# Twenty weight units multiplied by VectorE instead of TensorE, one matmul for the bias rows, and eight slots for the experts' weights

## What is computed

```python
mod = silu(c) @ w_ada + b_ada              # six passes of 3072 columns over the three blocks
h = modulate(rms_norm(x), shift, scale)
u, q, v, f_f, f_b, g = split(h @ w_in)     # the input layer, 3072 columns, partly for the context too
...                                        # Fourier mixing, and a gated recurrence in both directions
x = x + gate1 * (cat @ w_out)              # the output layer
aff = softmax(h @ w_router); idx = top_k(aff, 32)      # 16 experts, 32 tokens each
hid = silu(x[idx] @ w_g[e]) * (x[idx] @ w_u[e])        # 1024 x 2816 each
ye = hid @ w_d[e]                                      # 2816 x 1024
...                                        # second block: attention, spatial gating, feed-forward
...                                        # third block, two layers: attention with a bias of relative
                                           # positions (rel_bias[bucket(offset)]), short convolution
```

## Time and profile before

| | |
|---|---|
| median of three runs | 2391.78 us |
| the profiled execution: its time / its span | 2389.73 us / 2387.6 us |
| TensorE matmuls busy | 1858.6 us (78%) |
| VectorE busy | 735.8 us (31%) |
| ScalarE busy | 538.3 us (23%) |
| DMA moved | 760.52 MB, mean 319 GB/s |
| mean granted TensorE clock | 0.773 |

### The profile page before, as it was taken

One profiled execution on the slowest core, in us unless ns is written; L12 is line 12 of the kernel. 1 busy time (PEld: TensorE's weight loads), 2 busy tenths in 40 slices (PEclk: granted clock), 3 DMA queues, 4 the chain that ended last, 5 costly groups with the idle time before them and its releaser, 6 DMA issues.

```text
span 2387.6 us, 34411 instructions
## 1 busy us (share of the span) xinstructions
PE 1858.6 (78%) x14680; PEld 1126.4 (47%) x14680; DVE 735.8 (31%) x1170; ACT 538.3 (23%) x860; POOL 54.3 (2%) x70
## 2 busy tenths in 40 slices
PE   5999887676666666766676667667799999999897
PEld 3786752211221122112211211221788899988886
DVE  4216630000000000000000000010655786667767
ACT  3431221000000000000000000000474564464553
POOL 0005000000000000000000000000000000000000
PEclk8999987755665676566657755665899999999998
DMA  8757579999999999999999999999643555743531
GB/s 358 264 196 270 193 304 393 425 425 426 425 426 425 425 426 426 426 425 426 426 426 425 425 425 426 425 426 426 226 133 124 170 173 187 223 147 120 161 102 62
DMA packets 153198, 760.52 MB, mean 319 GB/s; under 512 B 9720, under 2 KB 96504, under 8 KB 99481
## 3 DMA queue, kind: packets, MB, share of 16 engines
q1 hardware_dynamic: 149448, 754.07, 79.2%
q10 hardware_dynamic: 3664, 5.24, 0.6%
HBM read 756.13 MB, written 3.14 MB: 318 GB/s over the span
## 4 chain that ended last, share of the span: by engine, by line
DMA 46%; PE 44%; DVE 5%; ACT 3%; issue 2%; SPq 0%; DVEq 0%; ACTq 0%
PE ps L633 17%; DMA ring<-in_w_exp_down 16%; DMA ring<-in_w_exp_up 15%; DMA ring<-in_w_exp_gate 14%; PE ps L897 7%; PE ps L1020 4%; PE ps L585 3%; PE ps L910 2%; PE ps L552 2%; DMA ring<-in_w_in 1%; PE ps L1002 1%; PE ps L783 1%; DVE ring_lo L1403 1%; PE ps L627 1%; PE ps L964 1%
## 5 line engine op out<-in xcount | busy, mean ns | idle before, releaser
L897 PE MATMUL ps<-ring,arena 128*32 128x352 f32 x4096 | 622.9, 755 | 241.1 <-DMA ring<-in_w_exp_gate 134.1
L897 PEld LDWEIGHTS ps<-ring,arena 128*32 128x32 f32 x4096 | 147.2, 153 | 703.5 <-DMA ring<-in_w_exp_up 257.8
L910 PE MATMUL ps<-ring,arena 128*32 128x256 f32 x2816 | 237.4, 492 | 176.5 <-DMA ring<-in_w_exp_down 129.9
L1403 DVE TENSOR_TENSOR ring_lo<-ring,w_hi 128x1024 fp32r<-128x1024 f32 x220 | 267.7, 1220 | 162.1 <-ACT w_hi L1060 161.0
L633 PE MATMUL ps<-u_hi,w_hi 128*128 128x258 f32 x960 | 278.3, 290 | 3.3 <-DVE ring_lo L1403 3.2
L633 PE MATMUL ps<-u_hi,ring_lo 128*128 128x258 f32 x960 | 272.4, 284 | 0.0
L633 PE MATMUL ps<-u_lo,w_hi 128*128 128x258 f32 x960 | 272.4, 284 | 0.0
L1748 DVE TENSOR_TENSOR arena<-arena,ps 128x704 f32<-128x704 f32 x15 | 13.3, 888 | 776.3 <-PE ps L897 776.3
L910 PEld LDWEIGHTS ps<-ring,arena 128*32 128x32 f32 x2816 | 99.5, 136 | 323.1 <-DMA ring<-in_w_exp_down 183.7
L1060 ACT ACTIVATE w_hi<-ring 128x1024 fp32r<-128x1024 f32 x220 | 230.3, 1050 | 92.7 <-PE ps L1020 36.2
L633 PEld LDWEIGHTS ps<-u_hi,w_hi 128*128 128x128 f32 x960 | 183.1, 191 | 14.4 <-DVE ring_lo L1403 8.8
(11 more groups left out here) (258 smaller groups left out, 1945.3 us busy)
## 6 DMA issues: line engine op xcount, KB each, us to landing
ring<-in_w_exp_gate SPq DMA_DIRECT2D x128, 1408.0 KB, 10.7
ring<-in_w_exp_up SPq DMA_DIRECT2D x128, 1408.0 KB, 10.9
ring<-in_w_exp_down SPq DMA_DIRECT2D x112, 1536.0 KB, 11.5
ring<-in_w_ada SPq DMA_DIRECT2D x48, 1536.0 KB, 8.7
ring<-in_w_in SPq DMA_DIRECT2D x38, 1536.0 KB, 7.2
ring<-in_w_ff SPq DMA_DIRECT2D x18, 1536.0 KB, 7.1
ring<-in_w_out SPq DMA_DIRECT2D x8, 1536.0 KB, 7.3
ring<-in_w_exp_down SPq DMA_DIRECT2D x16, 512.0 KB, 10.5
```

The lines of the kernel that those rows point to most:

```text
L897: m = pe.matmul(ps[32 * j:32 * j + 32, 2 * (k // 8) + i, 0:FJ // 2], XCUR[:, k % 8, :], ring[:, s, at:at + FJ // 2], start=(k % 8 == 0), s ...
L910: m = pe.matmul(ps[32 * j:32 * j + 32, 4, 0:T], HIDT[:, c, :], ring[:, s, at:at + T], start=(c == 0), stop=(c == FC - 1), skip_group_check ...
L1403: tt(slot(c["u"], KD, c["w"], of=ring_lo)[:, :, at], slot(c["u"], KD, c["w"])[:, :, at], w_hi[:, s % HI, :, :].bitcast(F32), ALU.subtract) ...
```

## The change

Three things change together.

**Twenty modulation units go to VectorE.** All of pass 1, all of pass 2 and four units of pass 3 (`DVE_ADA`) are loaded during the input layer, in slots 2 and 3 by turns, while the input layer's own units use slots 0 and 1 by turns. VectorE multiplies each element by the row's condition and adds it to an accumulator of 128 x 3072 (two instructions of 1536 columns a unit, in `add_ada`), right behind the low parts of the same item. `IN1_ADA` says how many such loads follow each of the input layer's units on SP. TensorE then sums each accumulator over the partitions with a matrix of ones, in eight matmuls of 384 columns (`ada_sum`): pass 1 behind item 10 of the input layer, pass 2 behind item 26, pass 3's part behind the layer. The turn of pass 1 comes behind item 12, that of pass 2 behind the layer. The other four units of pass 3 and pass 4 stay on TensorE, between the Fourier and the level steps; pass 5 follows the output layer.

**Bias rows.** One matmul makes all eight heads' rows on eight partitions, and each row is stored by a DMA that reads its one partition 128 times.

**Eight slots.** The experts' units go through eight slots: the four of the ring, one over the buffers of the high parts, three in a region whose data are no longer used by then. Experts' units 0 and 1 are issued ahead of most of pass 5. Slots are no longer `u % 4` but given by lists (`CYCLE`, `EXP_CYCLE`), and a load waits for the unit that had its slot before. The first load of in2 now has slot 0, whose last user is the experts' last unit but one. SP's loop over the experts is written out. The gating weights are loaded behind the experts, and their mask is applied in the second block.

```diff
-BROW_EVERY = 3
+SLOTS_ALL = 8
+CYCLE = (2, 3, 1, 0)
+EXP_CYCLE = (6, 7, 4) + CYCLE + (5,)
+IN1_ADA = [0, 2, 2, 1, 2, 2, 3, 3, 5]
+DVE_ADA = [(1, k) for k in range(KD)] + [(2, k) for k in range(KD)] + [(3, k) for k in range(4)]
+BROW_AT, SUM1_AT, TURN1_AT, SUM2_AT = 4, 10, 12, 26
+ADA_COND = (0, 0, 2, 2, 3, 3)
...
-    def unit(self, dmas=1):
+    def unit(self, dmas=1, by="unit_used", at=None):
+
         u = self.n
         self.n += 1
-        self.fill[u % RING] += 16 * dmas
-        self.ready[u] = self.fill[u % RING]
+        if at is None:
+            at = CYCLE[self.turn % RING]
+            self.turn += 1
+        self.where[u], self.before[u], self.last[at] = at, self.last[at], u
...
+        with nc.sbuf_tensor("w_hi_raw", [P, HI * KD * P], F32) as w_raw_t:
+            w_raw = w_raw_t[:]
         w_hi = sb("w_hi", [P, HI, KD, P], F32R)
...
+        ACC = (ar(0, 2 * ADA_J), tail[:, 0:2 * ADA_J])
+        SLOT = [ring[:, i, :] for i in range(RING)] + \
+            [w_raw[:, 0:UNIT], ar(4 * K1, UNIT), ar(20 * K1, UNIT), ar(23 * K1, UNIT)]
...
             def load(u, dst, src):
-                if u >= RING:
-                    sp.wait_ge(S("unit_used"), u - RING + 1)
-                sp.dma_start(dst, src).then_inc(w_ready[u % RING], 16)
+                if plan.before[u] is not None:
+                    name, n = plan.used[plan.before[u]]
+                    sp.wait_ge(S(name), n)
+                sp.dma_start(dst, src).then_inc(w_ready[plan.where[u]], 16)
...
             def after_in1(i):
-                if i < KD:
-                    load_ada(1, [i])
+                for _ in range(IN1_ADA[i]):
+                    p, k = next(dve_ada)
+                    load_ada(p, [k])
...
-            for p in (2, 3):
-                load_ada(p)
+            load_ada(3, range(4, KD))
+            load_ada(4)
             load_dense(out1, inp["w_out"][0])
-            for p in (4, 5):
-                load_ada(p)
+            load_ada(5, range(1))
...
+            sp.wait_ge(S(plan.used[out1[0]["u"]][0]), plan.used[out1[0]["u"]][1])
+            sp.wait_ge(S("bias_stored"), 16 * ATT)
+            load_expert(0)
+            load_expert(1)
+            load_ada(5, range(1, KD))
+            sp.wait_ge(S(plan.used[out1[-1]["u"]][0]), plan.used[out1[-1]["u"]][1])
+            for i in range(2, 7):
+                load_expert(i)
+            sp.wait_ge(S("xs"), KD)
+            for i in range(7, EXPERTS * EXP_UNITS):
+                load_expert(i)
...
+            def ada_sum(p):
+
+                pe.wait_ge(S("rows_out"), p)
+                pe.wait_ge(S("ada_used"), min(KD * p, len(DVE_ADA)))
+                for i in range(2):
+                    for j in range(CG):
+                        at = ADA_J * (j % 2) + ADA_J // 2 * i
+                        m = pe.matmul(ps[32 * j:32 * j + 32, 6 + i, 0:ADA_J // 2], ones[:, 0:32],
+                                      ACC[j // 2][:, at:at + ADA_J // 2], start=True, stop=(p < 3),
+                                      skip_group_check=True)
+                count(m, "ada_summed")
...
+            for i, _ in enumerate(dense_blocks(in1, in1_src, lat)):
+                if i == BROW_AT:
+                    pe.wait_ge(S("rel_in"), 32)
+                    m = pe.matmul(ps[0:ATT, 5, 0:511], REL[0:33, :], OFFS[0:33, 0:511], start=True, stop=True)
+                    count(m, "brow")
+                if i == SUM1_AT:
+                    ada_sum(1)
+                if i == TURN1_AT:
+                    turn(1)
+                if i == SUM2_AT:
+                    ada_sum(2)
+            turn(2)
+            ada_sum(3)
...
-                fill(2 if n < LEVELS - 1 else 0)
+                fill((1 + n % 2) if n < LEVELS - 1 else 0)
...
-                act.dma_start(scratch[h:h + 1, 0:P * 512].rearrange("a (q j) -> q (a j)", q=P)[:, 0:511],
-                              BROW[:, h % 2, 0:511]).then_inc(S(f"bias_stored{h % 2}"), 16)
+                act.dma_start(scratch[h:h + 1, 0:P * 512].rearrange("a (q j) -> a q j", q=P)[:, :, 0:511],
+                              BROW[h:h + 1, 0:511].unsqueeze(1).broadcast_to([1, P, 511])).then_inc(S("bias_stored"), 16)
...
+                    if BROW_AT < done <= BROW_AT + ATT:
+                        bias_row(done - BROW_AT - 1)
...
+            def add_ada(k):
+
+                for _ in range(k):
+                    p, kc = next(to_add)
+                    u = ada[p][kc]
+                    waits(f"w_ready{plan.where[u]}", plan.ready[u])
+                    c = conds[:, kc, ADA_COND[p]:ADA_COND[p] + 1]
...
+                    for i in range(2):
+                        w = slot(u, ADA_PASS)[:, 2 * ADA_J * i:2 * ADA_J * (i + 1)]
+                        if kc == 0:
+                            ins = ts(ACC[i], w, c, None, ALU.mult)
+                        else:
+                            ins = stt(ACC[i], w, c, ACC[i], ALU.mult, ALU.add)
+                    mark(ins, "ada_used")
+
+            done = 0
+            for gi, g in enumerate(in1):
+                share = IN1_ADA[gi + 1] if gi + 2 < len(in1) else (3, 2)[gi + 2 - len(in1)]
+                for i, it in enumerate(g["items"]):
                     low_parts(it["s"] + HI)
-
+                    n = len(g["items"])
+                    add_ada(share * (i + 1) // n - share * i // n)
+                    if done == TURN1_AT + 1:
+                        mod_in(1)
+                    done += 1
+            waits("ada_summed", 3)
```

More of the change, by code:

```diff
@@ L120, in __init__ @@
         self.ready = {}
-        self.fill = [0] * RING
+        self.fill = [0] * SLOTS_ALL
+        self.last = [None] * SLOTS_ALL
+        self.before = {}
+        self.where = {}
+        self.used = {}
+        self.counts = {"unit_used": 0, "ada_used": 0}
+        self.turn = 0
         self.blocks = 0
@@ L124, in __init__ @@
         self.splits = []
-    def unit(self, dmas=1):
+    def unit(self, dmas=1, by="unit_used", at=None):
         u = self.n
         self.n += 1
-        self.fill[u % RING] += 16 * dmas
-        self.ready[u] = self.fill[u % RING]
+        if at is None:
+            at = CYCLE[self.turn % RING]
+            self.turn += 1
+        self.where[u], self.before[u], self.last[at] = at, self.last[at], u
+        self.fill[at] += 16 * dmas
+        self.ready[u] = self.fill[at]
+        self.counts[by] += 1
+        self.used[u] = by, self.counts[by]
         return u
@@ L160, in dense @@
             k = 2 if inside else min(WCOL // P, end - n)
-            u = self.unit()
+            u = self.unit(at=at(len(units)))
             todo = [(n, which) for which in kinds(n)] if inside else \
@@ L164, in dense @@
                  for e in [(i, which) for which in kinds(i)] + [(name, t) for m, name in flips if m == i for t in range(NT)]]
-            at = [self.split(u, i * P, k * P) for i in range(k)]
-            assert not inside or at[0] % 2 == 0
+            parts = [self.split(u, i * P, k * P) for i in range(k)]
+            assert not inside or parts[0] % 2 == 0
             items = [self.block(u, i == len(todo) - 1, flip=m, t=which) if isinstance(m, str) else
-                     self.block(u, i == len(todo) - 1, n=m, turned=inside, src=which, col=(m - n) * P, s=at[m - n])
+                     self.block(u, i == len(todo) - 1, n=m, turned=inside, src=which, col=(m - n) * P, s=parts[m - n])
                      for i, (m, which) in enumerate(todo)]
@@ L264, in S @@
             return sems[name]
-        w_ready = [S(f"w_ready{i}") for i in range(RING)]
+        w_ready = [S(f"w_ready{i}") for i in range(SLOTS_ALL)]
         def sb(name, shape, dt=F32):
@@ L428, in col, with slot @@
             return cols[:, i, c:c + 1]
-        def slot(u, *shape, of=ring):
+        def slot(u, *shape, of=None):
             n = 1
@@ L479, in _ @@
             load_ada(0)
+            dve_ada = iter(DVE_ADA)
             def after_in1(i):
-                if i < KD:
-                    load_ada(1, [i])
+                for _ in range(IN1_ADA[i]):
+                    p, k = next(dve_ada)
+                    load_ada(p, [k])
                 if i == 2:
@@ L537, in unit_ready @@
             def unit_ready(u):
-                pe.wait_ge(w_ready[u % RING], plan.ready[u])
+                pe.wait_ge(w_ready[plan.where[u]], plan.ready[u])
             def count(ins, name):
@@ L546, in ada_unit @@
                 unit_ready(u)
-                if kc == 0 and p > 0:
+                first = (p, kc) in ((0, 0), (4, 0), (5, 0))
+                if first and p > 0:
                     pe.wait_ge(S("rows_out"), p)
@@ L709, in in1_src @@
                 return C_HI, C_LO
-            rest = dense_blocks(in1, in1_src, lat, lambda i: ada_unit(1, i) if i < KD else None)
             pe.wait_ge(S("mod_ready"), 1)
-            for h in range(ATT):
-                for _ in range(BROW_EVERY):
-                    next(rest)
-                pe.wait_ge(S("relb"), 1)
-                if h >= 2:
```

(20 more changed lines are left out.)

170 lines of the change are left out of this document (84 added, 86 removed).

## The result

The changed kernel is slower: 2441.15 us (median of 4, 2435.27 to 2448.81) against 2391.39 (4 runs, 2390.29 to 2393.57), a ratio of 1.0209 (95% interval 1.0179 to 1.0238). I had forecast 2385.0, with 2358 to 2412 as the range. The profiled execution took 2435.27 us, its span is 2433.1. That is 45.5 us more than the span of before, 2387.6; the medians are 49.8 us apart.

A forecast was written before the change was run, and what follows sets the result against it. The experts' weights were taken as a fixed block of bytes, so what counts is when their stream flows without a gap. +24.4 - 0.8 - 36.1 + 5.7 = -6.8 us, from 2391.8 to 2385.0; range 2358 to 2412.

The forecast's parts named there:

- Part 1: Input layer, TensorE: units and bias rows leave, three sums and a turn come in, -13.0 us.
- Part 2: Start of the input layer: in1[0]'s load waits for its new slot and lands 4.7 us later, 2.7 as lower end.
- Part 3: Input layer, VectorE and slot pairs: TensorE waits more; with all terms the Fourier part starts 24.4 us later (18 to 31).
- rival (A): Input layer: bias rows read from one partition hold the DMA engines, 0 to 52 us, time 2393 to 2437; chance 0.25.
- (a) to (d): TensorE's four waits in the input layer: 11.2 us at in1[3]'s second low part, 8.9, 7.1 and 3.5 at the three sums.
- The clock's term: Input layer: a lower granted clock after four longer waits costs +2.2 us, with 0 and 9 as ends.
- mostly ahead of work that VectorE paces: Input layer: the reason given for costing the clock after four longer waits at only +2.2 us together.
- Part 4: Fourier part to output layer: one unit fewer between Fourier matmuls gives -0.8 us; fewer units between levels win nothing.
- Part 5: Output layer to experts: fewer bytes to move, so the experts' unit 8 lands earlier, -36.1 us; eight loop slots cost nothing.
- Part 6: Behind the experts: in2[0] lands later from its new slot, +4.5 us, gating weights beside it +1.2; together +5.7.
- (B): Input layer: waits and the clock's share are a third, Fourier part starts at 186 us, time 2363; chance 0.25.
- (C): Whole kernel: a wash, 2387 to 2396 us; chance 0.08.

The follow-up runs named there:

- e1: The changed kernel with each bias row again computed for and stored from 128 partitions, at the same eight points: 2412.08 us, ratio 1.0061.
- e10: The changed kernel with its one-partition bias rows stored behind every third block instead of behind eight blocks in a row: 2436.75 us, ratio 1.0168.
- e2: The kernel before, with each bias row's store reading one partition 128 times: 2400.01 us, ratio 1.0027.
- e6: The changed kernel with bias rows stored once, then copied within DRAM, and in2[0] in the slot of the experts' unit 19: 2401.00 us, ratio 1.0025.
- e4: e1 with in2[0] in the slot of the experts' unit 19 instead of unit 22's: 2403.16 us, ratio 1.0032.
- e8: e6 with input-layer loads reordered, constants loaded behind in1[8], and sixteen units on VectorE, not twenty: 2365.02 us, ratio 0.9879.
- e5: The kernel before, with twelve 255.5 KB transfers from differing sources added behind its end, each alone: 3 to 12 us each.
- e9: e6 with input-layer loads reordered, constants loaded behind in1[8], and a unit's matmuls on constants added at four levels: 2384.23 us, ratio 0.9951.

## Why the prediction was wrong

**Part 1** held: 14.0 us of work left TensorE, forecast 13.0. **Part 2** held: +5.2, forecast +4.7.

**Part 3** failed, at the step "I wrote the four queues out in their order with these durations": a modulation unit's load lands 6.3 us after its issue or 3.7 behind the one ahead, one of in1 after 7.2. In the changed kernel the loads issued from 92 to 168 us landed after 15 to 26. The layer's waits, +30.5 in the sum, were +68.4. The step left out the eight stores on ScalarE's queue, whose source had changed; I had priced them, as rival (A), outside the sum. The rival was right in mechanism and place: rows at 29 GB/s, landings of 12.3 us, in1's loads over 12. Its price, 0 to 52 us, holds the 35 between e1 and the changed kernel, also with the 7 us of row matmuls that e1 has back; the time, 2441, is above its upper end of 2437. I had given it 0.25, on two arguments. "The other queue may pass them": it did so only in part, since the 16 engines are busy at 0.91 with 29 GB/s from 102 to 107 us, and at 0.93 with 96 GB/s from 108 to 114. "They are issued one per block": five came in two bunches, and e10 gives back some 10 of the 35 us for spacing them. What the prediction had in hand and did not join was its own part 3: a layer in which TensorE already waits for loads four times has little for eight slow transfers to lie beside. e2 shows the other half: in the kernel before the same stores cost some 6 us.

The rest of part 3 stood, as e1 shows: four waits of 11.6, 8.7, 7.5 and 4.0 us at the places and sizes of (a) to (d). A fifth, 5.2 us near 70 us where the kernel before has 2.9, was not in the sum. In e6, which has the changed kernel's one row matmul and is thus nearest to what I had summed, the four are 12.9, 10.5, 9.1 and 3.6. The price of a unit on VectorE too; by shape:

```profile
L1684 DVE SCALAR_TENSOR_TENSOR arena<-ring,conds,arena 128x1536 f32<-128x1536 f32 x17 | 30.9, 1817 | 25.9 <-DMA ring<-in_w_ada 25.8
...
L1682 DVE TENSOR_SCALAR arena<-ring,conds 128x1536 f32<-128x1536 f32 x3 | 3.1, 1019 | 5.4 <-DMA ring<-in_w_ada 3.5 <-PE ps L605 1.9
```

1.82 us where I had 1.83 from the slope. **The clock's term** was mis-sized: I took +2.2 with 9 as the upper end, and it is +10.6 in the changed kernel and +9.0 in e1. The step that failed is the discount "mostly ahead of work that VectorE paces": the one wait of the earlier trace rows cost 2.3 us by my estimate, and four at that price are 9.2, which is near what both runs show. No run tries the discount by itself. With that the forecast without the rows is 2392.

**Part 4**: +1.8 for -0.8. **Part 5** held: -33.9 here and -36.4, -36.9 and -36.1 in e1, e4 and e8, forecast -36.1. Its steps held too: counted from the output layer's start the experts' first matmul comes 16.5 us earlier than before (forecast 16.7), and their unit 8 lands 34.7 earlier. Eight slots in the loop cost nothing and win nothing: the same point of two experts is 81.33 us apart, as in the earlier trace rows.

```profile
904.47 23.39 DMA ring<-in_w_exp_gate
...
985.80 23.39 DMA ring<-in_w_exp_gate
```

**Part 6**: +7.3 for +5.7. in2[0] landed 8.5 us after its issue (forecast 7.2) and 7.7 behind the experts' end; e4 gives 4.9 back for one line.

**Rivals (B) and (C)** did not come. With the rows out of the way the kernel isn't at my 2385, a ratio of 0.997, either: e4 and e6, which have part 6 mended as well, are at 1.0032 and 1.0025. In e6's layer the waits are 6.5 us over my sum and the clock 5.2; between the levels its profile loses 19.1 us more to the clock than that of before, for which the sum had nothing, and in this the profiles differ widely.

## What to carry to other kernels

What a store that repeats its source costs is set by the partitions that it reads: the same 255.5 KB took 3 to 12 us in e5. Reading one partition 128 times in place of 128 computed rows saved 7 us of matmuls and still made the kernel 35 us slower, since it held the DMA engines that all queues share. A DMA share near 1 with few GB/s beside it is how a profile shows it. And the same eight slow transfers were worth some 6 us in the kernel in which TensorE has filler lying ready, and 35 in the one in which each load is the next thing needed: count what lies ready beside them, and not the engines' idle share.

## What the runs showed of the hardware that I had not expected

- At the same rate, one partition holds the engines and four neighbours don't. From 2399 to 2405 and from 2429 to 2436 us of e5, the single partition and partitions 0 to 3:

```profile
2399.00:2405.00 6.00, 0.00 (x0) 0.00 (x0) 0.00 (x0) 0.00 (x0) 0.00 (x0) 0.50 0.89 27
...
2429.00:2436.00 7.00, 0.00 (x0) 0.00 (x0) 0.00 (x0) 0.00 (x0) 0.00 (x0) 0.50 0.23 25
```

  A share of 0.89 and one of 0.23 for some 26 GB/s. In such windows inside the other forms the share goes by the number of source partitions, and is near a sixteenth for each: 0.13 and 0.12 for two, 0.23 and 0.24 for four, 0.46 and 0.47 for eight, 0.93 for sixteen. Only the form with one partition (0.89) holds all engines for 27 GB/s. Whether a store from four partitions would spare the loads beside it was not tried.
- The issue of a DMA can hold its queue for long: one row's issue on ScalarE's queue took 6.41 us. The other seven took 0.49 to 1.08, beside engines as busy, and in e1, which has no row from one partition, a load's issue on SP's queue took 5.95. So what makes an issue long is open.

```profile
118.34 1.72 ACTq L1198 DMA_DIRECT2D bias_rows<-arena  x2
120.13 6.41 ACTq L1198 DMA_DIRECT2D bias_rows<-arena  x1
```

- The granted clock between the levels differs from profile to profile of the same matmuls: the loss is 7.5 to 25.3 us in the six that have them. Four units' matmuls more did not lower it (19.5 in e9).
